# Reading 44 convolution taps from the transposition banks of PSUM instead of SBUF

## The reference

```python
xn = rms_norm_2(x, norm_mix)
proj = xn @ w_in                       # queries, keys, values, conv_in, q_mem, gates
kc = rms_norm_2(compress_blocks(k_c, cmp_pos[0], cmp_w1[0], cmp_w2[0]), nsa_qk_norm[1])
vc = compress_blocks(v_c, cmp_pos[1], cmp_w1[1], cmp_w2[1])
...
a, ag = jnp.split(conv_in, 2, axis=-1)
u = a * jax.nn.sigmoid(ag)             # 256 tokens x 512 channels
# u: causal depthwise convolution, 31 taps per channel, + conv_b
u = jax.nn.silu(layer_norm(u, conv_ln_g, conv_ln_b))
br_conv = u @ w_conv_out
```

## Time and profile before

| | us |
|---|---|
| median of 3 runs | 968.31 (967.64 to 971.62) |
| the profiled execution | 972.83 |
| its span, first to last instruction | 971.1 |
| TensorE busy | 893.0 (92%) |
| VectorE busy | 689.6 (71%) |
| ScalarE busy | 510.7 (53%) |
| GpSimd busy | 320.6 (33%) |

### The profile page before, as it was taken

The page is one execution under the profiler, slowest core; times in us unless marked ns, Lnnn a source line. Parts: engine busy times, 40 slices in busy tenths (PEclk is TensorE's granted clock), DMA queues, the critical chain, the costliest instruction groups (busy, mean ns, idle before and its releaser), DMA issues.

```text
span 971.1 us, 16923 instructions
## 1 busy us (share of the span) xinstructions
PE 893.0 (92%) x6718; PEld 850.5 (88%) x6718; DVE 689.6 (71%) x984; ACT 510.7 (53%) x926; POOL 320.6 (33%) x150
## 2 busy tenths in 40 slices
PE   4996779999999998889999489999996999999998
PEld 4985669999999998788989479988996999999998
DVE  6757742899889993768879998754677476566573
ACT  6377345654555556765756264446643544444441
POOL 4653103122233333253545451221343223223220
PEclk8997869999999998999999798899998999999999
DMA  5734004354565665361655242222354456656651
GB/s 190 280 112 150 22 2 115 107 181 149 168 206 177 204 183 154 91 191 62 208 158 166 111 152 66 87 87 66 101 161 130 125 159 197 187 176 184 189 153 44
DMA packets 54078, 137.18 MB, mean 141 GB/s; under 512 B 6000, under 2 KB 24816, under 8 KB 53872
## 3 DMA queue, kind: packets, MB, share of 16 engines
q1 hardware_dynamic: 54000, 136.11, 45.1%
HBM read 135.03 MB, written 1.05 MB: 140 GB/s over the span
## 4 chain that ended last, share of the span: by engine, by line
PE 77%; DVE 14%; issue 4%; ACT 4%; DMA 1%; SPq 0%; DVEq 0%; ACTq 0%
PE PROD L576 15%; PE PROD L577 14%; PE PROD L578 14%; PE SC L717 3%; PE OP L761 3%; DVE wlo L1491 3%; PE PROD L638 2%; PE OP L576 2%; PE OP L578 2%; PE OP L577 2%; PE SC L576 2%; PE SC L577 2%; PE SC L578 2%; PE TP L578 2%; PE TP L577 2%
## 5 line engine op out<-in xcount | busy, mean ns | idle before, releaser
L559 POOL TENSOR_TENSOR wlo<-raw,whi 128x1024 fp32r<-128x1024 f32 x124 | 316.7, 2561 | 626.8 <-ACT whi L1012 626.8
L576 PE MATMUL PROD<-HA,whi 128*128 128x256 f32 x1096 | 318.5, 291 | 10.4 <-DVE HA L1519 5.7
L577 PE MATMUL PROD<-HA,wlo 128*128 128x256 f32 x1096 | 314.3, 287 | 0.0
L578 PE MATMUL PROD<-HA,whi 128*128 128x256 f32 x1096 | 314.1, 287 | 0.0
L1012 ACT ACTIVATE whi<-raw 128x1024 fp32r<-128x1024 f32 x252 | 261.4, 1050 | 45.6 <-PE PROD L578 24.2
L1491 DVE TENSOR_TENSOR wlo<-raw,whi 128x1024 fp32r<-128x1024 f32 x128 | 183.1, 1434 | 102.9 <-ACT whi L1012 102.6
L576 PEld LDWEIGHTS PROD<-HA,whi 128*128 128x128 f32 x1096 | 214.8, 196 | 13.0 <-DVE HA L1519 6.1
L577 PEld LDWEIGHTS PROD<-HA,wlo 128*128 128x128 f32 x1096 | 214.9, 196 | 0.6 <-issue 0.6
L578 PEld LDWEIGHTS PROD<-HA,whi 128*128 128x128 f32 x1096 | 214.6, 196 | 0.0
L1906 DVE SCALAR_TENSOR_TENSOR CY<-U,CV,CY 128x255 f32<-128x255 f32 (+29 forms) x120 | 71.5, 670 | 0.2
L1773 DVE SCALAR_TENSOR_TENSOR YC<-Y,CV,YC 128x255 f32<-128x255 f32 x88 | 66.9, 763 | 2.2 <-ACT YC L1206 0.7
(11 more groups left out here) (316 smaller groups left out, 1707.7 us busy)
## 6 DMA issues: line engine op xcount, KB each, us to landing
raw<-stream SPq DMA_DIRECT2D x208, 512.0 KB, 3.9
raw<-stream SPq DMA_DIRECT2D x136, 128.0 KB, 2.4
raw<-stream SPq DMA_DIRECT2D x8, 384.0 KB, 3.1
raw<-stream SPq DMA_DIRECT2D x8, 256.0 KB, 3.3
X<-xT SPq DMA_DIRECT2D x2, 512.0 KB, 5.1
E<-memT SPq DMA_DIRECT2D x1, 1024.0 KB, 5.8
out<-X SPq DMA_DIRECT2D x8, 128.0 KB, 2.0
PX<-pT SPq DMA_DIRECT2D x1, 256.0 KB, 3.8
```

Of the source, the lines that this page charges most:

```text
L559: nc.gpsimd.tensor_tensor(wlo[:, n % NSPLIT, :], raw[:, n % NRAW, :], whi[:, n % NSPLIT, :].bitcast(F32), ALU.subtract).then_inc(lo_pool, 1)
L576: nc.tensor.matmul(dst, wh, hi, start=start, stop=False, skip_group_check=True)
L577: nc.tensor.matmul(dst, wl, hi, start=False, stop=False, skip_group_check=True)
L578: last = nc.tensor.matmul(dst, wh, lo, start=False, stop=stop, skip_group_check=True)
```

## The change

Chunks 0 and 1 of `U` are written twice: to SBUF as before, and by a second instruction to `UT`, a view of the PSUM tensor `TP`. The first 44 taps read `UT` instead of `U`; they still read and write `CY` in SBUF. The second instruction waits until the sums of `down` in that bank were read. Besides, the places of some tiles move: ScalarE makes the upper halves of tiles up to 141 right after the roots of `qm0` and `qm1`, and VectorE makes only the tiles below 142 between `qm0` and `qm1` and the rest up to 143 after the four taps.

```diff
--- before.py
+++ after.py
@@ -249,6 +249,7 @@
 MEMK_AT = {2: 0, 4: 1}
 MEM_SCALE = P ** -0.5
 BIAS_STEP = 6
+EARLY_TAPS = 44
 
 
 def bases(pairs):
@@ -352,6 +353,7 @@
         MEMX = E0[:, :, :].rearrange("p h n -> p (h n)")[:, 0:DC * S].rearrange("p (c s) -> p c s", c=DC)
         VM = SQ[:, 0:4, :].rearrange("p c s -> p (c s)").rearrange("p (q n) -> p q n", q=QT)
 
+        UT = TP[:, :].rearrange("p (c s) -> p c s", c=4)
         UU = Y[:, 4:8, :].rearrange("p (a b) s -> p a b s", a=2)
         GT = OMEM[:, 0, :].rearrange("p (k s) -> p k s", k=2)
 
@@ -1340,6 +1342,7 @@
 
             root("qm0", P, 2 * S)
             root("qm1", P, 2 * S)
+            weights(FIRST["cmpk"] // BPT + NSPLIT + 2)
 
             def nsa_gate(o, m):
                 wait_product(act, o)
@@ -1900,10 +1903,11 @@
                         dve.wait_ge(vchain, at_tap[c])
                     w = COL["conv_w_2"] + c * KSIZE + k
                     shift = KSIZE - 1 - k
+                    src = UT[:, c, :] if done["taps"] < EARLY_TAPS else U[:, c, :]
                     if shift == 0:
-                        ins = nc.vector.tensor_scalar(CY[:, c, :], U[:, c, :], CV[:, w:w + 1], None, ALU.mult)
+                        ins = nc.vector.tensor_scalar(CY[:, c, :], src, CV[:, w:w + 1], None, ALU.mult)
                     else:
-                        ins = nc.vector.scalar_tensor_tensor(out=CY[:, c, shift:S], in0=U[:, c, 0:S - shift],
+                        ins = nc.vector.scalar_tensor_tensor(out=CY[:, c, shift:S], in0=src[:, 0:S - shift],
                                                              scalar=CV[:, w:w + 1], in1=CY[:, c, shift:S],
                                                              op0=ALU.mult, op1=ALU.add)
                     ins.then_inc(vchain, 1)
@@ -1917,6 +1921,10 @@
                 wait_product(dve, o)
                 ahead(o)
                 wait_freed(dve, ("conv2", 2 * c + 1))
+                if c < 2:
+                    wait_freed(dve, ("down", 4 + 2 * c + 1))
+                    nc.vector.scalar_tensor_tensor(out=UT[:, c, :], in0=TH[:, c % 2, :], scalar=1.0,
+                                                   in1=product(o)[:, 0:S], op0=ALU.add, op1=ALU.mult)
                 nc.vector.scalar_tensor_tensor(out=U[:, c, :], in0=TH[:, c % 2, :], scalar=1.0,
                                                in1=product(o)[:, 0:S], op0=ALU.add, op1=ALU.mult).then_inc(free(o), 1)
                 wait_freed(dve, o)
@@ -1939,10 +1947,9 @@
                 last.then_inc(qm_normed, 1)
                 dve.wait_ge(qm_normed, i + 1)
                 if i == 0:
-                    wait_product(dve, ("cmpk", 1))
-                    ahead(("cmpk", 1))
+                    weights(FIRST["cmpk"] // BPT + NSPLIT + 2)
             conv_taps(4)
-            for o in (("gnsa", 0), ("cmpv", 1)):
+            for o in (("cmpk", 1), ("gnsa", 0), ("cmpv", 1)):
                 wait_product(dve, o)
                 ahead(o)
             maxima(UNITS2[0], MEM_SCALE)
```

## The result

Timed side by side, the kernel before takes 972.37 us (median of 20 executions, 967.64 to 985.15), the changed kernel 965.69 us (median of 20, 961.43 to 979.63). The ratio is 0.9942, 95% interval 0.9917 to 0.9966. The change is faster by 6.7 us of medians, where 11.5 were predicted, and 965.69 lies above the range's end of 963.5. Of the miss of 8.9 us, 4.1 lie in the base, which was 968.31 in three executions and 972.37 in twenty; 4.8 lie in the gain. The ratios and the means further down leave out executions more than 1.5% above the fastest of their kernel. The profiled execution took 968.41 us, its span 966.7.

The account below looks back on a forecast made before the run. TensorE was taken to wait 12.4 us for tile 140, late on VectorE behind taps held by GpSimd. Scores 10.7 us earlier plus 0.8 in the first unit gave 11.5: 968.31 - 11.5 = 956.8 us, range 952.0 to 963.5.

Parts of the forecast that it names:

- The 40 taps escape GpSimd: VectorE before `qm0`: 40 taps reading PSUM avoid GpSimd contention, 31.35 us becoming 15.5; rival that they are held, 0.09.
- A tap from PSUM costs no more: VectorE taps: reading PSUM adds zero time per tap; rival of slower PSUM reads, 0.028 us a tap, 0.04.
- The reciprocal of `qm0` at 528.8: VectorE after the 40 taps: this reciprocal moves from 543.41 to 528.8 us, 14.6 us earlier.
- `QN` collision: Second scaling of `QN` on VectorE: could meet GpSimd's start at 508.83 us and be held 2.2 us.
- Tile 140 at 537.5, TensorE stalls for 0.9 us: Second tile of `cmpv`: ready between 534.3 and 540.3 us, taken as 537.5, against TensorE's need at 536.6.
- Tile 143 is what is late next: Before `gnsb` 0: tile 143 comes at 544.6 us, TensorE waits 2.9 us, scores end 10.7 us earlier.
- 0.8 us in the first unit: First unit's 14 taps, still from `U`: GpSimd tiles running earlier free 0 to 3 us, taken as 0.8.
- Part 4, ScalarE's tiles before the GELU: ScalarE makes high halves of tiles 140 and 141 before table load and GELU, holding the GELU about 0.3 us.
- What is saved before 577 us moves all that comes later: After the stretch: TensorE is busy all the time from 600 us, so earlier savings carry through.
- I take the stretch as the same in both: Profiled execution (972.83 us) and median (968.31 us) share the same stretch, so 11.5 us comes off both.
- The range's end, 963.5: Whole kernel: upper end of the range, meant to take in both ends of the collisions and PSUM price.
- 960.4: Whole kernel time under the rival that collisions take more: scores 7.9 us earlier, up to 963.5; chance 0.14.

Follow-up runs that it names:

- tile 143 early: The changed kernel with tile 143 put back between `qm0` and `qm1` on VectorE; 964.72 us (0.9905), again 966.82 us (0.9933).
- taps alone: The changed kernel without the moved tiles, only the 44 taps from PSUM; 964.39 us (0.9931), 965.21 us (0.99), 968.25 us (0.9932).
- taps alone with one and with two reciprocals: Taps alone plus one or two full unused VectorE reciprocals ahead of the second reciprocal; one 963.39 us (0.9906), two 966.04 us (0.9928).
- change with one: The changed kernel plus one full unused VectorE reciprocal (3.3 us) ahead of the second reciprocal; 971.48 us (0.997).

## Why the prediction missed

Times after are set against 496.31 and 495.91, the first `U` of each trace, so that 0.4 us is taken off each gain.

- **The 40 taps escape GpSimd**: right. 15.6 us, forecast 15.5; one tap each 0.38 us with GpSimd at work beside it. The gap that was named, the scalar from `CV` in SBUF, does not matter: these taps read one and were not held. The Trainium skill (GPSIMD Engine Reference, Specifications) names VectorE instructions with two SBUF inputs or in a two-port mode; the trace agrees.
- **A tap from PSUM costs no more**: right. 14 taps took 5.47 us from `TP`, 5.26 and 5.42 from `U`. The Trainium skill (VectorE: DVE Perf Modes, the TRN2 errata section) gives 120 fixed cycles for a PSUM source and 58 for an SBUF one. The runs do not show the difference for taps in a row.
- **The reciprocal of `qm0` at 528.8**: 530.14, or 530.5 with the start evened out. The 1.7 us are the `QN` collision of 2.15 us, which stood in the text and not in the sum. The other three traces of the change have this reciprocal 1.5 us later behind the first `U` (35.7 for 34.2 us).
- **Tile 140 at 537.5, TensorE stalls for 0.9 us**: 538.84 and 1.0 us, inside 534.3 to 540.3. In the other three traces it would stand at 540.7 to 540.9, just beyond the bound, so the good agreement of the first is in part luck.
- **Tile 143 is what is late next**: right, 2.6 us of wait for 2.9. Its refill makes ScalarE wait 2.9 us more. The first exponentials came 8.0 us earlier (562.50 to 554.13) instead of 9.9.
- **0.8 us in the first unit**: too little. Its 14 taps take 5.26 us for 11.60, and the exponentials of the second memory unit, the next point, come at 566.34 for 577.20, 10.5 us earlier.
- **Part 4, ScalarE's tiles before the GELU**: wrong in sign. Without it tile 140 is done 1.0 us earlier than in the first trace of the change and 2.5 to 2.7 earlier than in the others, counted from the first `U`. By the times it costs nothing that was measured.
- **"What is saved before 577 us moves all that comes later"**: this step failed. The row it rests on has TensorE busy for 60 of 60 us, and its clock column reads 0.89. A full busy column was read as full speed. TensorE bounds that part, but up to a quarter of its time runs at half speed (16 to 56 us), and how much does differs from kernel to kernel and between executions of one kernel. In the first pair of traces TensorE's busy time there grew by 8.4 us and the part by 6.4.
- **"I take the stretch as the same in both"**, with the median of three as base: the base moved by 4.1 us with more executions. From 972.37 the forecast gain would have given 960.9, and 965.69 would still have been 4.8 us above. But the range, moved up with the base, would end at 967.6 and hold the time.
- **The range's end, 963.5**: too low by the prediction's own terms. 960.4 with the 2.2 us at 509 us and one more block of 2.4 us is 965.0.

The account by the table: the stretch gave 79.4 - 69.9 = 9.5 us (mean of the changed kernel's four traces), the rest took 898.8 - 894.1 = 4.7 back, and 973.5 - 968.7 = 4.8 are left. With both traces of before (77.8) it is 7.9 and 3.1. That the change itself lengthens the later part is argued from these means and not shown: the kernel before has 204.1 us there in one trace and 213.8 in the other, the changed one 210.6 to 216.4. What sets the series of falls was not found. Shown is that it is not a late tile 143 and not idle time in the stretch alone, and that TensorE's load in the 11.8 us before does not tell the two cases apart.

## What to carry to other kernels

Where GpSimd and VectorE work side by side, move one input of VectorE's many small instructions to an idle bank of PSUM: it halved their time here and freed GpSimd too. Tiles moved in the same edit undid a third of the gain here (2.5 of 7.3 us), so trace each part alone. Where the bound engine's granted clock is below 1 in the part that follows, count a saving as gained only for the stretch itself and leave some per mille of the time open on both sides for what follows. Take the base from many executions: three gave 968.31 us here, twenty 972.37.

## What the runs showed of the hardware

- A tap with both tensors in SBUF and GpSimd's subtraction hold each other: 18 taps take 17.49, 17.60 or 11.22 us for 6.85, and GpSimd's tile 3.7 us for 2.4. With one input in PSUM both run at their own speed (0.38 us a tap, 2.4 us a tile).
- TensorE's granted clock falls to its lower level also where the engine is busy without a gap (60.00 of 60 us at 0.89). The same later part took 202.4 to 216.4 us, with 16 to 56 us of it at 1.2 GHz.
- The series of falls can repeat to a microsecond between executions of one kernel (both of tile 143 early, the first and third of the taps alone, the second and fourth of the change) and can differ (the other traces of the last two, both of the kernel before). Four kernels with different edits (tile 143 early, taps alone with one and with two reciprocals, change with one) share the falls at 23, 40, 57 and 173 us, to a microsecond.
- Ahead of the stretch, where the programs are the same, the first `U` came between 494.1 and 503.4 us in the 18 traces. Kernels of this length can't be compared by one execution each.
